# Expert weights of a mixture-of-experts layer issued from two queues instead of one

## The reference

```
logits = xf @ router_w + router_b            # (256, 32)
top_v, top_i = top_k(logits, 4); gate = softmax(top_v)
for each expert e, for its tokens xs:
    h = xs @ w1[e] + b1[e]                   # 1024 -> 2048: gate half and up half
    g = minimum(h[:, :1024], 7);  u = clip(h[:, 1024:], -7, 7)
    y = ((u + 1) * g * sigmoid(1.702 * g)) @ w2[e] + b2[e]     # 1024 -> 1024
    out[token] += gate * y
x = layer_norm(alpha * x + out)
```

## Time and profile before

| | |
|---|---|
| median of 3 runs | 1282.0 us (1280.66 to 1282.93) |
| the profiled execution, its time | 1280.4 us |
| its span | 1278.3 us |
| mean granted TensorE clock | 0.987 |
| TensorE busy | 1206.2 us, 94% |
| VectorE / ScalarE / GpSimd busy | 301.6 / 217.6 / 27.7 us |
| DMA moved | 429.77 MB, 336 GB/s over the span |
| of it on SyncE's queue | 427.56 MB |
| the chain that ended last | TensorE 67%, DMA 22%, VectorE 6% |

### The profile page before, as it was taken

The page is one execution under the profiler, slowest core; times in us unless marked ns, Lnnn a source line. Parts: engine busy times, 40 slices in busy tenths (PEclk is TensorE's granted clock), DMA queues, the critical chain, the costliest instruction groups (busy, mean ns, idle before and its releaser), DMA issues.

```text
span 1278.3 us, 15327 instructions
## 1 busy us (share of the span) xinstructions
PE 1206.2 (94%) x6263; PEld 557.0 (44%) x6263; DVE 301.6 (24%) x742; ACT 217.6 (17%) x428; POOL 27.7 (2%) x37
## 2 busy tenths in 40 slices
PE   7999999999899999999999999999999999999995
PEld 6875889795533333333333333333333333333331
DVE  1344757552511111111111111111111111111113
ACT  2233434341111111111111111111111111111111
POOL 1001010100000000000000000000000000000000
PEclk9999999999799999999999999999999999999998
DMA  9324000007889999999999999999999999999995
GB/s 334 141 99 151 1 1 1 1 1 271 371 353 426 428 431 428 428 427 369 427 431 429 428 427 430 429 429 427 429 430 429 427 429 430 429 427 429 430 428 216
DMA packets 42236, 429.77 MB, mean 336 GB/s; under 512 B 4844, under 2 KB 10035, under 8 KB 17507
## 3 DMA queue, kind: packets, MB, share of 16 engines
q1 hardware_dynamic: 40656, 427.56, 79.9%
q10 hardware_dynamic: 1267, 1.02, 0.4%
q0 software_dynamic: 288, 0.85, 0.2%
HBM read 428.36 MB, written 1.05 MB: 336 GB/s over the span
## 4 chain that ended last, share of the span: by engine, by line
PE 67%; DMA 22%; DVE 6%; ACT 2%; POOL 1%; issue 1%; ACTq 0%; SPq 0%; DVEq 0%
PE bank L1165 26%; DMA ring<-in_exp_w 22%; PE bank L1195 12%; PE bank L831 5%; PE bank L1137 3%; PE bank L841 3%; PE bank L989 2%; PE bank L1003 2%; PE bank L1002 2%; PE bank L1146 2%; PE bank L1085 2%; PE bank L1184 1%; DVE pool L1670 1%; DVE pool L1665 1%; DVE pool L1667 1%; ACT pool L781 1%
## 5 line engine op out<-in xcount | busy, mean ns | idle before, releaser
L1165 PE MATMUL bank<-ring,pool 128*64 128x512 f32 x1280 | 288.8, 596 | 10.8 <-DMA ring<-in_exp_w 10.8
L1195 PE MATMUL bank<-ring,pool 128*64 128x512 f32 x1024 | 226.8, 595 | 0.0
L1165 PE MATMUL bank<-pool 128*64 128x512 f32 x768 | 174.6, 596 | 0.0
L1165 PEld LDWEIGHTS bank<-ring,pool 128*64 128x64 f32 x1280 | 87.9, 137 | 194.1 <-issue 171.3
L1195 PEld LDWEIGHTS bank<-ring,pool 128*64 128x64 f32 x1024 | 70.5, 137 | 154.0 <-issue 154.0
L1651 DVE TENSOR_SCALAR pool<-pool 128x128 f32<-128x128 f32 x64 | 19.3, 345 | 420.7 <-PE bank L1165 420.7
L1663 DVE TENSOR_SCALAR pool<-bank 128x512 f32<-128x512 f32 x32 | 22.2, 692 | 330.7 <-PE bank L1165 330.7
L1165 PEld LDWEIGHTS bank<-pool 128*64 128x64 f32 x768 | 51.8, 136 | 106.6 <-issue 106.6
L1137 PE MATMUL bank<-pool 64*128 64x512 f32 x264 | 65.6, 614 | 0.7 <-ACT pool L785 0.7
L1123 PE MATMUL bank<-pool 128*64 128x512 f32 x264 | 62.3, 592 | 1.1 <-DVE pool L1629 1.1
L785 ACT ACTIVATE pool<-bank 128x512 f32<-128x512 f32 x32 | 19.2, 598 | 250.4 <-PE bank L1195 250.4
(11 more groups left out here) (276 smaller groups left out, 939.7 us busy)
## 6 DMA issues: line engine op xcount, KB each, us to landing
ring<-in_exp_w SPq DMA_DIRECT2D x144, 2048.0 KB, 19.8
pool<-in_exp_w SPq DMA_DIRECT2D x48, 2048.0 KB, 25.0
ring<-in_w_in SPq DMA_DIRECT2D x4, 2048.0 KB, 9.3
ring<-in_w_out SPq DMA_DIRECT2D x2, 2048.0 KB, 7.7
ring<-in_w_in SPq DMA_DIRECT2D x2, 1536.0 KB, 13.3
pool<-in_consts SPq DMA_DIRECT2D x1, 1665.0 KB, 20.0
ring<-in_w_in SPq DMA_DIRECT2D x1, 1632.0 KB, 6.6
pool<-in_x SPq DMA_DIRECT2D x1, 1024.0 KB, 5.4
```

The costliest lines, as they stand in the source:

```text
L1165: last = mm(bank[4 + g][hp, :], lhs, w[:, k % 2, o:o + 512], start=False, stop=(k == KD - 1))
L1195: last = mm(bank[6][SLOTS * hf:SLOTS * hf + SLOTS, :], hT[:, k % 4, SLOTS * (k // 4):SLOTS * (k // 4) + SLOTS], w2s[k // 4][:, k % 4, 512 ...
```

## The change

SyncE keeps q0 to q2 of every expert (`first_parts`), now in one loop without the switch at `AHEAD`. `last_parts` moves to GpSimd with its waits: q3 and both halves of w2 of every expert leave from GpSimd's queue. Of expert 0, q3 and the second half of w2 are issued by GpSimd behind the wait for `s_ot`, and the first half behind the wait for `s_grp`, ahead of the two memsets.

```diff
--- before.py
+++ after.py
@@ -495,33 +495,16 @@
                     sp.wait_ge(s_w1, it * 4 + (q - 7))
                     load_slot(e, q, odd)
 
-            def last_parts(e, it):
-
-                sp.wait_ge(s_w1, it * 4)
-                load_slot(e, 3, False)
-                for q in range(4, 6):
-                    sp.wait_ge(s_w2, it * 2 + (q - 5))
-                    load_slot(e, q, False)
-
-            def from_second(it0):
-
-
-                with sp.Fori(0, AHEAD // 2) as e2:
+            def from_third(it0):
+
+                with sp.Fori(0, NE // 2 - 1) as e2:
                     for odd in range(2):
                         e = e2 * 2 + odd
                         first_parts(e + 2, it0 + e + 2, odd)
-                        last_parts(e + 1, it0 + e + 1)
-                last_parts(AHEAD + 1, it0 + (AHEAD + 1))
-                with sp.Fori(AHEAD // 2, NE // 2 - 1) as e2:
-                    for odd in range(2):
-                        e = e2 * 2 + odd
-                        first_parts(e + 2, it0 + e + 2, odd)
-                        last_parts(e + 2, it0 + e + 2)
 
 
             sp.wait_ge(s_ot, NP)
-            for q in (2, 3, 5):
-                load_slot(0, q, False)
+            load_slot(0, 2, False)
 
             sp.wait_ge(s_grp, 7)
             for i, name in enumerate(("ln1_g", "ln1_b")):
@@ -531,7 +514,6 @@
             for g in range(2):
                 sp.dma_start(bias[NE * g:NE * g + NE], t["exp_b1"][0][:, F * g:F * g + F]).then_inc(s_bias, 16)
             sp.dma_start(bias[2 * NE:3 * NE], t["exp_b2"][0]).then_inc(s_bias, 16)
-            load_slot(0, 4, False)
             load_slot(1, 0, True)
             sp.wait_ge(s_mix, 4)
             for q in (0, 1):
@@ -540,16 +522,15 @@
             load_slot(1, 1, True)
             sp.wait_ge(s_lg, 1)
             load_slot(1, 2, True)
-            from_second(0)
+            from_third(0)
 
             sp.wait_ge(s_moe, 2)
             npass = sp.value_load(npass_i[0:1, 0:1], min_val=1, max_val=MAXPASS)
             with sp.If(npass > 1):
                 with sp.Fori(1, npass) as p:
                     first_parts(0, p * NE, False)
-                    last_parts(0, p * NE)
                     first_parts(1, p * NE + 1, True)
-                    from_second(p * NE)
+                    from_third(p * NE)
 
             sp.wait_ge(s_gts, npass * NE)
             for i, name in enumerate(("ln2_g", "ln2_b")):
@@ -1245,9 +1226,30 @@
                     nc.gpsimd.tensor_tensor(xmT[:, d], m, x2.unsqueeze(1).broadcast_to([P, 4, P]), ALU.mult).then_inc(s_gps, 1)
                 mask_factors(2 * pt)
                 mask_factors(2 * pt + 1)
+            pool.wait_ge(s_ot, NP)
+            pool.dma_start(w1s[3], ew1[0][3]).then_inc(s_slot[3], 16)
+            pool.dma_start(w2s[1], ew2[0][1]).then_inc(s_slot[5], 16)
             pool.wait_ge(s_grp, 7)
+            pool.dma_start(w2s[0], ew2[0][0]).then_inc(s_slot[4], 16)
             nc.gpsimd.memset(gT, 0.0).then_inc(s_zero, 1)
             nc.gpsimd.memset(ysb, 0.0).then_inc(s_yev, 1)
+
+            def last_parts(e, it):
+
+                pool.wait_ge(s_w1, it * 4)
+                pool.dma_start(w1s[3], ew1[e][3]).then_inc(s_slot[3], 16)
+                for h in range(2):
+                    pool.wait_ge(s_w2, it * 2 + (h - 1))
+                    pool.dma_start(w2s[h], ew2[e][h]).then_inc(s_slot[4 + h], 16)
+
+            with pool.Fori(1, NE) as e:
+                last_parts(e, e)
+            pool.wait_ge(s_moe, 2)
+            npass = pool.value_load(npass_i[0:1, 0:1], min_val=1, max_val=MAXPASS)
+            with pool.If(npass > 1):
+                with pool.Fori(1, npass) as p:
+                    with pool.Fori(0, NE) as e:
+                        last_parts(e, p * NE + e)
 
 
         @block.vector
```

## The result

| | before | after |
|---|---|---|
| median | 1281.83 us (4 runs, 1280.66 to 1282.93) | 1297.07 us (4 runs, 1295.29 to 1297.98) |
| ratio | | 1.0121, 95% interval 1.0105 to 1.0138 |
| profiled execution, its time and span | 1280.4, 1278.3 us | 1297.98, 1296.1 us |
| lost to waits in the expert loop | 13.6 us | 27.2 us |

What follows compares the result with a forecast made beforehand. PE bounds the first experts (28.16 us each), DMA the later ones (29.37). Equal queue shares make PE 24.9 us late instead of 13.6, other terms adding nothing: 1282.0 + 11.3 = 1293.3 us, range 1276 to 1314.

Steps and rivals of the forecast that it cites:

- (a), nothing on the issue side: Expert-load issue: same 192 loads, 96 now issued by otherwise idle POOL; zero on the path.
- (b), the hole goes: SP's loop: the order switch and its slow DMA stretch go; worth at most 4.6 us if order of need stayed.
- (c), the prologue is the same to me: Before expert 0: same loads go out, small SP loads even earlier; zero.
- (d), half each: Expert loop: two queues with work share the engines equally, so a 4.89 us load takes twice that when shared.
- (d), the sum of waits: Expert loop: w2's second half is late from expert 9; PE 24.9 us late at the end instead of 13.6, +11.3.
- a late start of 2 us alone: Start of POOL's loads: first wait two experts earlier, +2 us; within the rival of POOL starved or late, chance 0.12.
- The end: Last experts: SP's last load some 40 us before POOL's, loads through near 1250, experts 30 and 31 at PE's pace.
- POOL with more than half: Expert loop rival: SP's third quarter is late from expert 18 or so, 14 waits, +3.4 us; chance 0.10.
- POOL with less: Expert loop rival: POOL late from the third or fourth expert, 28 waits, +20 us, up to 1302; chance 0.12.
- a fuller: Whole-loop rival: two queues keep engines fuller; about +0 at 435 GB/s, −7 us at 440; chance of faster 0.15.
- the slower rival: Whole-loop rival: two queues or POOL's descriptors lower the DMA rate; at 420 GB/s about +25 us, 1307; chance 0.08.

Runs made afterwards that it cites:

- small tensors first: Changed kernel, but GpSimd's loads of both w2 halves of expert 0 wait until the small tensors have landed; 1295.15 us, ratio 1.0117 to the kernel before.
- the exchange: Changed kernel with queues swapped: SyncE issues q3 and the w2 halves, GpSimd q0 to q2, small tensors first; 1293.02 us, ratio 1.0105 to the kernel before.
- e5_sp8k: Changed kernel, but SyncE's quarters are loaded as two DMAs of 8 KB rows each; 1294.24 us, ratio 1.0124 to the kernel before.
- e6_pool8k: Changed kernel, but GpSimd's q3 and w2 halves are loaded as two DMAs of 8 KB rows each; 1310.47 us, ratio 1.0235 to the kernel before.
- run 27: Not a run's number: "in the run 27 waits" counts the 27 waits in e6_pool8k, which took 1310.47 us.
- e9_q3_only: Changed kernel, but only q3 leaves from GpSimd; SyncE issues q0 to q2 two experts ahead, then w2's halves; 1290.96 us, ratio 1.0086 to the kernel before.

## Why the prediction was right, point by point

It forecast +11.3 us (1293.3); measured were +15.2 (1297.07), inside its range and on its side. The path was right; the sum was too small in two places, one before the loop and one in it.

- **(a), nothing on the issue side**: right. GpSimd's issues took 0.53 us each on an engine that had nothing else to do.
- **(b), the hole goes**: right, no slice below 427 until the end, and the waits show no gain from it; that this is because order of need had gone is argued.
- **(c), the prologue is the same to me**: this step failed. I costed the small loads at zero because less stood ahead of them in their own queue, and did not count the other queue, against which their rows go one for one. It cost 2.8 us (the difference from 54.5 to 57.3, undone by small tensors first).
- **(d), half each**: right. The Trainium skill's rule (DMA: Bandwidth & Descriptors, Queues, rings and completion order) that an engine alternates between its queues a packet at a time is borne out, with the row as the unit: 7.4 us against 9.8 for a load when the other queue's rows were half as long.
- **(d), the sum of waits**: mechanism right, size 2.3 us short, 24.9 forecast and 27.2 measured. The term that was too small is the start of a load. The sum put start and landing together at 2.8 us, taken from loads of one queue, and added it once, at the end; a load whose queue was empty began at once. In the trace the last row is followed by the landing within 1.1 us, but q3 of experts 1 to 4, which find GpSimd's queue empty (expert 4's but for 0.1 us) and SyncE's at work, each begin 3.5 to 3.6 us after their issue. The last row of the second half of w2 of experts 1 to 5 is through at 390.4, 421.0, 451.6, 482.1 and 512.1 (the changed kernel's times less 4.1 us, the later start of its loop), where the prediction has 387.8, 418.5, 448.5, 477.5 and 508.8. The same sum with a start of 3.6 us for such loads of GpSimd and 3.45 for SyncE's, and 1.0 for SyncE's first, gives 391.4, 421.9, 452.4, 482.9 and 512.3, an estimate, but it leaves less than 1 us open at each expert. So expert 5 has a margin of 2.2 us instead of 3.9, and the first wait comes two experts early. The prediction had this price in its rivals ("a late start of 2 us alone brings the first wait forward by two experts, +2"), as a fault of GpSimd's loads; it is one of two queues, as the exchange shows. No run takes the start away alone. (Redone as it stands, the sum has 479.2 where it says 477.5; by expert 5 this makes no difference.)
- **The end**: right. SyncE's last load was issued at 1209.6, GpSimd's at 1255.0, DMA was done early, and the last two experts ran at TensorE's pace.

13.6 us in the loop and 2.8 before it make 16.4, and the two profiled spans differ by 17.8; the other 1.3 is the earlier part of that execution, and that part moves by up to 5.6 us from profile to profile. The medians differ by 15.2. The two terms that were too small, 2.8 and 2.3, make 5.1 us, and the forecast is only 3.9 us short of the medians; the 1.2 us between lie in what differs from execution to execution, and are luck.

The rivals: POOL with more than half was made by e5_sp8k, and did move the waits to SyncE's third quarter, at expert 14 rather than 18. POOL with less was made by e6_pool8k: 28 waits and +20 in the prediction; in the run 27 waits, 39.0 − 13.6 = 25.4 us more in the loop, 5 or so of it from the lower rate, and 31.0 us more in all. Neither a fuller nor a slower DMA came of the second queue with 16 KB rows: 427 to 429 GB/s in the changed kernel's slices. The Trainium skill's rule on engines 7 and 15 (same page, Latency and other measured facts), on which the slower rival leant, is not seen in the rate of any run here with 16 KB rows; no view here shows the DMA engines one by one.

## What to carry to other kernels

This stage was at the DMA's rate. The second queue added no bandwidth and took away the one thing that a single queue gives for nothing, the order of need; pieces with one buffer then waited behind pieces that were needed an expert later. Before splitting loads, count for each queue how much of the engines it gets (here row for row, so long rows won over short ones), what slack its buffers have, and what a load pays that starts an empty queue beside a busy one. If there is a hole in a single queue, mend its order instead: here that gave 0.24% where the split cost 1.2%.

## What the runs showed of the hardware

- Two queues shared by rows, not bytes: with 16 KB rows on both, GpSimd's loads began 9.8 us apart; with 8 KB rows on SyncE's, 7.4. Rows of 4 KB and 128 bytes beside 16 KB rows landed 5 us later though two loads of 2 MB had been taken from ahead of them.
- A load that started an empty queue sent its first row 1.0 us (SyncE) or 1.25 us (GpSimd) after the issue with nothing else under way, and 3.3 to 3.8 us after it while the other queue's rows were going out: 31 of e9_q3_only's 32 loads of q3 took 3.65 to 3.8 us, and SyncE's in e6_pool8k 3.4 to 3.5.
- Rows of 8 KB on one of the two queues, either one, lowered the rate of the loop from 429 to 425 GB/s.
- Behind two waits of 4.0 us TensorE's granted clock was 0.5 for 3.4 and 6.8 us (e5_sp8k), behind one of 2.2 us for 3.4 us (e9_q3_only).
